# High products whose 512 moving columns are read in alternating runs of 16, and 96 unused products behind the last group

## The reference

```python
h = rmsnorm(x, norm_mix[l]);  p = h @ w_in[l]            # 2048 x 4608
y_b = diff_attention(q, k, v, ...)                       # 8 heads
y_a = multiscale_pool(a_in, ...)
y_c = conformer_conv(c_in, ...)
x = x + concat([y_b, y_a, y_c]) @ w_out[l]               # 2048 x 2048
h = rmsnorm(x, norm_ffn[l]);  gu = h @ w_ffn_in[l]       # 2048 x 11008
g = causal_dwconv(gu[..., :D_FF], ...)
x = x + (silu(g) * gu[..., D_FF:]) @ w_ffn_out[l]        # 5504 x 2048
```

## Time and profile before

| | |
|---|---|
| median of 3 runs | 2080.03 us (2079.98 to 2080.92) |
| span of the profiled execution | 2078.2 us |
| granted TensorE clock | 0.998 |
| PE busy | 2064.8 us, 99% |
| DVE busy | 1415.6 us, 68% |
| ACT busy | 1081.7 us, 52% |
| HBM read | 389.43 MB |

### The profile page before, as it was taken

How to read it: one execution, slowest core, us unless ns; L and a number is a source line. 1 busy time by engine, 2 the same in 40 slices (tenths; PEclk the granted TensorE clock), 3 DMA queues, 4 the chain that set the end, 5 groups by cost and what they waited for, 6 DMA issues and landing times.

```text
span 2078.2 us, 32569 instructions
## 1 busy us (share of the span) xinstructions
PE 2064.8 (99%) x11564; PEld 1792.4 (86%) x11564; DVE 1415.6 (68%) x2009; ACT 1081.7 (52%) x1509; POOL 23.5 (1%) x20
## 2 busy tenths in 40 slices
PE   9999999999999999999999999999999999999998
PEld 8888888888888888888888888888888888888886
DVE  7998777676666666555489978676666676654454
ACT  6556655555555554433374566455555555544444
POOL 0001100000000000000000011000000000000000
PEclk9999999999999999999999999999999999999999
DMA  8554455655555555555666544655555655565664
GB/s 290 179 183 159 139 183 182 204 190 192 192 182 192 191 192 193 193 197 179 207 209 196 177 145 145 198 190 192 191 184 182 202 189 195 183 212 193 194 199 163
DMA packets 108944, 392.66 MB, mean 189 GB/s; under 512 B 12225, under 2 KB 12737, under 8 KB 108481
## 3 DMA queue, kind: packets, MB, share of 16 engines
q1 hardware_dynamic: 106992, 386.45, 56.6%
q10 hardware_dynamic: 1872, 5.13, 0.8%
HBM read 389.43 MB, written 2.10 MB: 188 GB/s over the span
## 4 chain that ended last, share of the span: by engine, by line
PE 99%; DMA 0%; DVE 0%; ACT 0%; ACTq 0%; issue 0%; DVEq 0%
PE bank L1179 53%; PE bank L1182 27%; PE bank L1458 4%; PE bank L1457 4%; PE bank L1456 4%; PE bank L1266 2%; PE bank L1255 1%; PE bank L1256 1%; PE bank L1257 1%; DMA x<-xT 0%; PE bank L1319 0%; PE bank L1431 0%; PE bank L1342 0%; DVE xt L1131 0%; DVE wlo L716 0%; ACT whi L364 0%
## 5 line engine op out<-in xcount | busy, mean ns | idle before, releaser
L736 DVE TENSOR_TENSOR wlo<-raw,whi 128x1024 fp32r<-128x1024 f32 x728 | 885.8, 1222 | 609.5 <-ACT whi L406 608.6
L1179 PE MATMUL bank<-xg,whi 128*128 128x512 f32 x3648 | 1135.6, 393 | 1.9 <-DVE wlo L716 1.9
L406 ACT ACTIVATE whi<-raw 128x1024 fp32r<-128x1024 f32 x728 | 764.2, 1057 | 693.3 <-PE bank L1182 558.0
L1182 PEld LDWEIGHTS bank<-xg,wlo 128*128 128x128 f32 x3648 | 685.0, 188 | 151.3
L1182 PE MATMUL bank<-xg,wlo 128*128 128x256 f32 x3648 | 720.1, 279 | 0.0
L1179 PEld LDWEIGHTS bank<-xg,whi 128*128 128x128 f32 x3648 | 552.9, 188 | 6.3 <-issue 3.3
L1179 PE MATMUL bank<-hidden,whi 128*128 128x512 f32 x688 | 213.5, 392 | 0.0
L1179 PE MATMUL bank<-mix,whi 128*128 128x512 f32 x512 | 160.7, 395 | 0.0
L1182 PEld LDWEIGHTS bank<-hidden,wlo 128*128 128x128 f32 x688 | 129.2, 188 | 28.5
L1182 PE MATMUL bank<-hidden,wlo 128*128 128x256 f32 x688 | 135.8, 279 | 0.0
L1456 PE MATMUL bank<-whi,hidden 128*128 128x512 f32 x344 | 134.6, 391 | 0.0
(11 more groups left out here) (150 smaller groups left out, 1140.8 us busy)
## 6 DMA issues: line engine op xcount, KB each, us to landing
raw<-wstream SPq DMA_DIRECT2D x729, 512.0 KB, 3.4
pw_sb<-pww ACTq DMA_DIRECT2D x2, 1024.0 KB, 7.3
outT<-xt SPq DMA_DIRECT2D x8, 256.0 KB, 2.9
x<-xT SPq DMA_DIRECT2D x2, 512.0 KB, 10.3
gains<-gain_rows ACTq DMA_DIRECT2D x1, 1024.0 KB, 6.3
raw<-wstream SPq DMA_DIRECT2D x2, 256.0 KB, 4.5
x<-xT ACTq DMA_DIRECT2D x2, 256.0 KB, 5.4
x<-xT SPq DMA_DIRECT2D x2, 256.0 KB, 7.3
```

Of the source, the lines that this page charges most:

```text
L406: nc.scalar.activation(whi[:, s, :], raw[:, s, :], ACT.Copy).then_inc(hi_ready, 1)
L736: nc.vector.tensor_tensor(wlo[:, s, :], raw[:, s, :], whi[:, s, :], ALU.subtract).then_inc(lo_ready, 1)
L1179: nc.tensor.matmul(ps[bank][:], whi[:, s, blk * P:blk * P + P], mov, start=first, stop=False)
L1182: return nc.tensor.matmul(ps[bank][:, 0:S], wlo[:, s, blk * P:blk * P + P], mov[:, 0:S], start=False, stop=last)
```

## The change

`high_product` now gives its moving operand and its output a pattern of 16 blocks, 2 halves and 16 columns: it reads 16 high columns, then 16 low ones, then the next 16 high ones, and writes the bank in the same order. The same columns are multiplied and land in the same places. `RUN` is 16. `low_product` and the products of `v_group` and `token_group` are as before.

Behind the last group PE issues four probes of 12 high and 12 low products each, in the same order of pairs (high, high, low, low). They take their moving columns from `hidden1`, write banks 0 to 3, and nobody reads the result. The first two probes read 512 columns in one run, from element 8 and from element 24; the other two read from element 16 in alternating runs of 4 and of 64. Before them stands a wait for `evacuated` at groups 0 and 1 of the stage.

```diff
--- before.py
+++ after.py
@@ -93,6 +93,7 @@
 assert sum(TAPS_AT.values()) == (CONV_K - 1) * NT
 
 WARM = 6
+RUN = 16
 COLS = NT * P
 FRONT = 3 * COLS
 STORES = ((1, 0), (0, 0), (1, 1), (1, 2), (0, 1), (0, 2), (1, 3), (0, 3))
@@ -1176,7 +1177,12 @@
             for l in range(LAYERS):
                 hidden = hidden_of[l]
                 def high_product(bank, s, blk, mov, first):
-                    nc.tensor.matmul(ps[bank][:], whi[:, s, blk * P:blk * P + P], mov, start=first, stop=False)
+                    nc.tensor.matmul(in_runs(ps[bank][:], RUN), whi[:, s, blk * P:blk * P + P], in_runs(mov, RUN),
+                                     start=first, stop=False)
+
+                def in_runs(columns, n):
+
+                    return columns.rearrange("p (h b t) -> p b h t", h=2, t=n)
 
                 def low_product(bank, s, blk, mov, last):
                     return nc.tensor.matmul(ps[bank][:, 0:S], wlo[:, s, blk * P:blk * P + P], mov[:, 0:S],
@@ -1478,6 +1484,22 @@
                               (lambda k: pe.wait_ge(hidden_ready, l * FFG + k // NT + 1) if k % NT == 0 else None)
                               if u == 0 else None, rel0=D0 + DP * u, hook=False)
 
+            flat = hidden1[:].rearrange("p k c -> p (k c)")
+            probes = [(8, None), (24, None), (16, 4), (16, 64)]
+            pe.wait_ge(evacuated, (LAYERS - 1) * TILES + TD + 8 + CREDIT)
+            for off, n in probes:
+                for pair in range(6):
+                    blks = (2 * (pair % 2), 2 * (pair % 2) + 1)
+                    for blk in blks:
+                        mov = flat[:, off:off + 2 * S]
+                        out = ps[blk][:]
+                        if n:
+                            mov, out = in_runs(mov, n), in_runs(out, n)
+                        nc.tensor.matmul(out, whi[:, 3, blk * P:blk * P + P], mov, start=True, stop=False)
+                    for blk in blks:
+                        nc.tensor.matmul(ps[blk][:, 0:S], wlo[:, 3, blk * P:blk * P + P], flat[:, off:off + S],
+                                         start=False, stop=True)
+
     assert SEEN == STEPS, (SEEN, STEPS)
```

## The result

| | before | after |
|---|---|---|
| median | 2080.01 us | 2158.26 us (2157.91 to 2158.66, 4 runs) |
| span of the profiled execution | 2078.2 us | 2156.5 us |

The ratio is 1.0374, with a 95% interval of 1.036 to 1.0389: slower by 78 us, twelve times the 6.5 us that were forecast, and past the upper end of the range (2130 us).

What follows compares the result with a forecast made beforehand. PE was taken as the bound, never waiting, its time being matmul count times start distance. 2080.03 + 6.45 (probes) + 0 (reading order) = 2086.5 us, range 2032 to 2130 us.

Steps and rivals of the forecast that it cites:

- The bound: Whole kernel: PE never waits, so time is matmul count times start distance, about 229 ns high and 116 low.
- The probes: Behind the last group: 48 high and 48 low added products, partly covered by the tail, lengthen the span by 6.45 us.
- The reading order: In the 4848 high products: alternating runs of 16 columns add 0 us to the sum, with -63 to +63 us possible.
- the unchanged pace: High products keep their distance, so only the added products behind the last group cost time: 2086.5 us, chance 38%.
- The step of "6.6 ns": Per high product: difference by where operands lie, 233 against 227 ns; times 4848 it makes 32 us.
- The upper bound: Worst case for the high products: their surplus over the columns doubles, 13 ns more each, 63 us.
- The low products: Low products read one run as before, so 0 change; at most one 6.6 ns step each if high ones affect them.
- More stalls: slower: High products: column and weight readings meet more, or jumps cost part of a cycle; 2118.5 us, up to 2150, chance 25%.
- Fewer stalls: High products: column and weight readings meet less in SBUF; one step gives 2054.5 us, whole surplus 2023, chance 34%.
- the bank in pieces: High products' output written in pieces is slow: 203 ns more each, about 985 us, 3071 us in all, chance 3%.
- The two ports: PE's two independent SBUF read ports: placement would not matter, sum stays at +6.45; the trace disagreed by 6 ns a product.

Runs made afterwards that it cites:

- p1_kinds: Twelve streams of 24 unused high products behind the kernel before, varying start, run length, and reading or writing in runs: 228.8 to 251.7 ns a product.
- p2_places: Thirteen streams of 24 unused high products behind the kernel before, varying places of columns and weights, half distances and blocks left out; runs of 16, weights moved: 240.0 ns.
- p4_strides: Ten streams of 24 unused high products behind the kernel before, reading every 6th to 17th block or halves 32 to 35 blocks apart: 226.7 to 242.1 ns.
- e4_write_only: Against the kernel before: high products write the bank in runs of 16 but read their columns in one run; 2080.22 us, ratio 1.0001.
- e5_run32: Against the kernel before: runs of 32 in all high products, no probes; 2119.15 us, ratio 1.0186.
- e8_not_in_turn: Against the kernel before: 4452 high products alternate every 16 columns between areas 512 elements (32 blocks) apart, no probes; 2090.36 us, ratio 1.0048.

## Why the prediction was wrong

**The bound** was right: PE's chain, the distances of 229 and 116 ns, no waits, DVE and ACT with room (after, DVE waits 665.2 us at the same place, ACT 632.0).

**The probes**: forecast 6.45 us, measured 7.15 and 7.05. The pace of 345 ns was taken for all; the trace of the changed kernel has 348 and 353 ns for the probes that read in one run from elements 8 and 24, and 372 for the runs of 4. From the first probe's start to the last one's end it was 17.2 us where the forecast had 2084.65 - 2067.93 = 16.7, and the 0.24 us of semaphores behind the last product were left out.

**The reading order** is the step that failed: "I take **0** for the sum, because the number of columns is the same and each run is 16 columns, 64 bytes, at its old place, and none of the rows favours one sign". It measured 71.0 us: a high product and its low one together took 15 ns longer, because the high product passes the places of its 64-byte blocks in the order 0,0,1,1,2,2,3,3 instead of 0,1,2,3. The rows did hold a hint against a zero, and the text named it (the 233 and 227 ns of the earlier trace rows, and "well under half" for the unchanged pace): the distance depends on places at the grain of 64 bytes, and the change altered the order at this very grain. A changed pace did get 59% of the chance, split between the two signs, but the sum took the middle. (The step of "6.6 ns" is 233.0 - 226.7 = 6.3 by its own rows; settled streams later gave 6.7.)

**The upper bound** was nearly right for the high product by itself: "the surplus doubles, a like 13 ns more"; it measured 11 (240 against 229), 53 us. But the range did not keep it. "I keep -63 and +63 us for the range" would have reached 2150 us; the range given ended at 2130, 43.5 us over the sum, or 9 ns a high product.

**The low products** were set to 0, with one step as a bound that then entered neither the range nor a rival. They cost 120 against 116 ns, 4848 x 4 = 19 us, a quarter of the loss, without a change to their own reading. 53 + 19 = 72, beside the 71.0 measured.

**The rivals.** "More stalls: slower" (25%) had the sign and, in half a sentence ("the columns stay in one place for twice as long"), part of the mechanism; its partner, the weights' reading, was not shown to be it (with 32 columns of weights the 240 ns are as they were), and its second guess, a price for each jump, is refuted (by the kernel with areas 33 blocks apart, 2080.03 us, and by every 5th block). "Fewer stalls" and the bank in pieces are refuted by 2151.32 and 2080.22 us.

**The two ports.** Of the Trainium skill's rule (TensorE: Matmul & The Clock Gate, "Step-by-step: what each phase is for"), that loading weights takes nothing from the running matmul, the streams bear out one half: in the slow order neither the place nor the width of the weights changes the 240 ns. In the quick order the other half fails: 227 ns with the weights from element 0, 233 with the weights from 16 or 8.

**What stays open.** Why four places, which part of the chip they are, whether a weight load has to be under way, why the low products lose 4 ns beside runs of 16 and nothing beside runs of 32, and why the order 0,0,1,1,2,2,3,3 costs 13 ns in a stream and 0,0,2,2 only 7. The settled distances 226.7, 233.3 and 240.0 ns are, by an estimate at 2.4 GHz, 544, 560 and 576 cycles: 32, 48 and 64 over the 512 columns. The runs show the order and its price, not the circuit.

## What to carry to other kernels

When fp32r columns stream at one a cycle, the order in which their 64-byte blocks pass four places 64 bytes apart (a period of 256 bytes) sets 6% of the pace (240 against 226.7 ns); let each block be in the place after the last one's, and jumps are free, even one every 16 columns. This was seen with 4-byte columns and blocks of 16; shorter runs cost more (252 ns for runs of 4). A strided or interleaved moving operand should be tested by the distance between starts in a stream of unused products, reading and writing apart, before it goes into the main loop; the stream tells slow from quick, but not the price in the kernel (30 us foretold, 10 measured). And where a trace shows that a pace depends on placement at some grain, a change of order at that grain should not be forecast as neutral.

## What the runs showed of the hardware

- A high product of 512 fp32r columns takes 227 ns in the quick order and 240 with blocks of 16 alternating between halves 1024, 1088, 1152 or 2048 bytes apart; runs of 4 columns, 1024 apart, make it 252, runs of 64 leave it at 229 (p1_kinds, p2_places).
- In one run the start counts too: 227 ns with columns and weights both from element 0, 229 with the columns from 16, and 233 with the columns from 8 or 24, or with the weights from 8 or 16 (p1_kinds, p2_places).
- Every 5th, 9th, 13th or 17th block of 64 bytes is as quick as every one; every 3rd or 7th 238, every 2nd or 6th 240, every 4th or 8th 242 ns (p2_places, p4_strides).
- Writing the bank in 32 runs of 16 costs nothing (2080.22 us, e4_write_only).
- A low product, which reads in one run, takes 120 ns in place of 116 when the high ones beside it read in runs of 16. It does not with runs of 32 (115 ns, e5_run32), nor with areas 32 blocks apart (115, e8_not_in_turn), though the high ones are slower there too.
